# Six stage borders: the low part of the third tile's weights made by GpSimd in place of VectorE

## The chip, the cores and the metric

The kernel runs on one core of a Trainium2 chip. The metric is the device time of one launch in microseconds (us). Of the core's engines four compute here: TensorE (PE) multiplies matrices, VectorE (DVE), ScalarE (ACT) and GpSimd (POOL) work elementwise; SyncE (SP) issues transfers of weights. Each engine takes its instructions in order, and they wait for each other through semaphores.

## What is computed

Four layers of a diffusion backbone over 256 context and 256 latent tokens of 1024 features, in float32. Each layer has a token mixer (neighbourhood attention, retention, convolution, attention again) and a channel mixer, and ahead of each of these eight sub-layers stands a norm with a shift and a scale:

```python
for i in range(DEPTH):                       # 4 layers, D_MODEL = 1024
    hx = modulate_norm(xs, norm_mix[i], mx[0], mx[1])
    hc = modulate_norm(cs, norm_mix[i], mc[0], mc[1])
    yx, yc = mixer(hx, hc)                   # attention, retention or convolution
    xs = xs + mx[2] * yx
    hx = modulate_norm(xs, norm_ffn[i], mx[3], mx[4])
    xs = xs + mx[5] * conv_ffn(hx, ...)      # the same for cs, with mc
# modulate_norm: x * rsqrt(mean(x*x) + eps) * gain * (1 + scale) + shift
```

## The kernel before

**Products.** Features lie on the partitions, in 8 chunks of 128, and all 512 tokens in the columns: context CT (0 to 255), latent XT (256 to 511). For float32 precision each product is three: high weights by high activations (L718), high by low (L719), low by high (L720). The weights are streamed in groups of 128x1024 through four slots (`raw`, `Whi`). For each group ScalarE copies the rounded high part, Whi (L1230, semaphore `hi_split`), and VectorE subtracts it from the raw weights, Wlo (L1599, semaphore `lo_split`), in place: Wlo lies over raw. Both engines do so three groups ahead of TensorE (LEAD = 3). TensorE waits for `lo_split` ahead of each group.

**Borders.** A border is the change from one sub-layer's last projection to the next one's first tiles, with the residual sum and the norm between. Sub-layers are numbered r = 0 to 7. `HALVED = (0, 2, 1, 1, 1, 2, 1, 0)` says how many of the last output tiles of the projection ahead of r are made in halves, first all context columns, then the latent ones: it is so at the six borders r = 1 to 6. There the context tokens are normalised while TensorE still works on the latent halves.

TensorE (`last_halves`, then `three_tiles`): the next sub-layer's first two tiles for the context tokens, chunk by chunk (k = 0 to 7, six products of 256 columns each, each chunk behind `h_ready`); after k = 4 it sums the latent tokens' squares (`norm_sum`, L839 and L843), after k = 6 it spreads their roots over the partitions (`norm_spread`, L898), for which it needs VectorE's diagonal. Then it waits for `lo_split` of the third tile's weights, makes that tile for the context tokens, and goes on with the latent columns.

VectorE (`norm_halves`, `normed_chunks`): for each chunk c of a stream the product ring = X * scale * root (L1696, the root read from PSUM), and behind the product of chunk c + 1 the low part of chunk c, Hlo = ring + shift - Hhi (L1687, ring and Hhi in SBUF). Between the products of chunks 5 and 6 of the context tokens stands the split of the third tile's weights. Behind the context chunks come `invert_root(r, XT)` (reciprocal L1660, diagonal L1663) and the eight latent chunks.

ScalarE (`norm_apply`): the high parts Hhi (L1278) of chunks 2, 3, 4, then the high part of the third tile's weights, then the chunks 5 to 7 and the root of the sums (L1269).

GpSimd (`after_residual`): squares (L577) and adds up (L579) the chunks of X as they come; during the channel mixers of three layers it multiplies conditioning weights (`scale_weights`, L585), at the fourth border it goes on with filters of the convolution (`taps_diagonal`, L677), at the sixth with loads of the attention bias.

Of the kernel before, what the change touches and what calls it, by code (L numbers as in the profile page):

```python
# [24 lines left out]
F32 = mybir.dt.float32  # L25
F32R = mybir.dt.float32r
ALU = mybir.AluOpType
# [5 lines left out]
C = D // P  # L33
# [36 lines left out]
LEAD = 3  # L70
# [16 lines left out]
HALVED = (0, 2, 1, 1, 1, 2, 1, 0)  # L87
# [107 lines left out]
def build(nc, x, ada, weights, ada_in, ada_bias, gain, na_gain, rpb, na_mask, rope, decay, dist, gn_gain,  # L195
          cv_bias, cv_filter, quad, ffn_filter, ones, head_ones, identity, out):
    layers, n_groups = plan()
    ctx = ExitStack()
    with ctx:
        def sb(name, shape, dt=F32):  # L200
            return ctx.enter_context(nc.sbuf_tensor(name, shape, dt))

        def sem(name):
            return ctx.enter_context(nc.semaphore(name))
# [5 lines left out]
        Whi = sb("Whi", [P, SLOTS, GROUP], F32R)  # L210
# [3 lines left out]
        Wlo = sb("Wlo", [P, SLOTS, GROUP], F32R)  # L214
# [102 lines left out]
        x_loaded = sem("x_loaded")  # L317
        hi_split = sem("hi_split")
        lo_split = sem("lo_split")
        weights_used = sem("weights_used")  # L320
        tile_free = sem("tile_free")
        c_loaded = sem("c_loaded")
# [109 lines left out]
        def ctx_first(r):  # L432
            return sum(HALVED[:r])
# [5 lines left out]
        def norm_tokens(layer, part):  # L439

            return XT if layer == DEPTH - 1 and part == 1 else ALL
# [6 lines left out]
        def token_blocks(tok):  # L448
            return (2, 3) if tok == XT else (0, 1) if tok == CT else (0, 1, 2, 3)

        def spread_bank(r, tok):
            return bank[7 if HALVED[r] and tok == XT else 5]

# [10 lines left out]
        def weighed(n):  # L464
            return 2 * (n + 1) - shared_before(n + 1)
# [102 lines left out]
        def _(pool):  # L568
            g = nc.gpsimd

            def clear_total(r, tok):
                pool.wait_ge(norm_summed, upto(r - 1, XT))
                g.memset(total[:, tok], 0.0).then_inc(sum_step, 1)

            def add_square(r, nth, c, tok):

                g.tensor_tensor(square[:, c % 2, tok], X[:, c, tok], X[:, c, tok], ALU.mult).then_inc(sum_step, 1)  # L577
                pool.wait_ge(sum_step, sum_first(r) + 2 + 2 * nth)
                g.tensor_tensor(total[:, tok], total[:, tok], square[:, c % 2, tok], ALU.add).then_inc(sum_step, 1)  # L579

            def scale_weights(n, per=0, i=0):

                pool.wait_ge(cond_weighed, weighed(n) + per * i)
                w = cond_w[:, n % COND_SLOTS, :]
                g.tensor_tensor(w, w, cond[:, 0, :], ALU.mult).then_inc(cond_scaled, 1)  # L585

            def after_residual(r, tile0, tok):

                clear_total(r, tok)
                whole = C - 1 - (HALVED[r] == 2)  # L590
                for c in range(whole):
                    pool.wait_ge(tile_free, FREE0 + tile0 + 1 + c)
                    add_square(r, c, c, tok)
                if whole == C - 2:
                    pool.wait_ge(ctx_added, ctx_first(r) + 1)
                    add_square(r, whole, whole, CT)
                    pool.wait_ge(tile_free, FREE0 + tile0 + 1 + whole)
                    add_square(r, whole + 1, whole, XT)
# [47 lines left out]
            for layer, p in enumerate(layers):  # L646
                r = 2 * layer
                if layer % 3 == 0:
                    pairs_staged(layer)
                    out_tile = p["mix_tile"] + 24  # L650
                elif layer % 3 == 1:
                    def add(dst, a0, b0):
                        return g.tensor_tensor(dst, decay_t[:, 0, a0:a0 + CTX], decay_t[:, 1, b0:b0 + CTX], ALU.add)

                    for h in range(RET_HEADS):
                        if h:
                            pool.wait_ge(mask_made, 6 * h)
                        else:
                            pool.wait_ge(rope_step, 17)
                        g.dma_start(decay_t[:, :, :], dist).then_inc(dist_loaded, 16)  # L660
                        pool.wait_ge(decayed, 2 * h + 2)
                        for b, (left, right) in enumerate((((P, 3 * P), (3 * P, P)), ((0, 2 * P), (2 * P, 0)),
                                                           ((P, 3 * P), (0, 2 * P)))):
                            if h >= 2:
                                pool.wait_ge(ret_out, 3 * (h - 2) + b + 1)
                            add(A[h % 2][b][:, CT], *left).then_inc(mask_made, 1)
                            add(A[h % 2][b][:, XT], *right).then_inc(mask_made, 1)
                    pool.wait_ge(ret_out, 3 * RET_HEADS)
                    out_tile = p["mix_tile"] + 48
                else:  # L670
                    pool.wait_ge(norm_summed, upto(r, XT))
                    g.dma_start(quad_in[:, :], quad).then_inc(quad_loaded, 16)
                    g.memset(U[:, :, :, 0:CONV_PAD], 0.0).then_inc(pads_cleared, 1)
                    g.memset(U[:, :, :, CTX + CONV_PAD:], 0.0).then_inc(pads_cleared, 1)
                    pool.wait_ge(quad_loaded, 16)
                    for c in range(C):
                        g.tensor_tensor(taps_diagonal[:, c, :, :],  # L677
                                        quad_one.unsqueeze(1).to_broadcast([P, 4 * MOST, QUAD]),
                                        quad_w[:, c, :].unsqueeze(2).to_broadcast([P, 4 * MOST, QUAD]), ALU.mult)\
                            .then_inc(diag_made, 1)  # L680
                    for c in range(C):
                        for n in range(len(pool_taps[c]) - 1):
                            i = added_before[c] + n
                            pool.wait_ge(product_made, i + 1)
                            if n == 0:
                                pool.wait_ge(pool_begun, c + 1)
                            else:
                                pool.wait_ge(pool_added, i)
                            g.tensor_tensor(pooled[:, c % 2, :], pooled[:, c % 2, :], products[:, i % PRODUCTS, :],
                                            ALU.add).then_inc(pool_added, 1)  # L690
                    for c in range(1, 4):
                        pool.wait_ge(ln_square, c + 1)
                        if c > 1:
                            pool.wait_ge(ln_added, c - 1)
                        g.tensor_tensor(total[:, :], total[:, :], LN_SQUARES[c], ALU.add).then_inc(ln_added, 1)
                    pool.wait_ge(ln_used, 1)
                    out_tile = p["mix_tile"] + 16
                after_residual(r + 1, out_tile, norm_tokens(layer, 1))
                if p["hosts"]:
                    with pool.Fori(0, FC // 2) as i:  # L700
                        for q in range(PER_LAP):
                            scale_weights(p["cond_up"] + q, PER_LAP, i)
                if layer < DEPTH - 1:
                    after_residual(r + 2, p["down_tile"], ALL)


        @block.tensor
# [886 lines left out]
        def _(dve):  # L1594
# [7 lines left out]
            def split(st):  # L1602

                st = st.ahead(LEAD)
                if not isinstance(st.n, int) or st.n < n_groups:
                    split_group(st)
# [138 lines left out]
            def norm_halves(r, tiles, add_half, following):  # L1745


                for n, c in enumerate(tiles):
                    dve.wait_ge(ctx_made, ctx_first(r) + n + 1)
                    add_half(c, bank[c % 4], 0, CT, ctx_added)  # L1750
                if r % 2:
                    split(following[0])
                norm_scale(r)
                invert_root(r, CT)
                if len(tiles) == 2:
                    dve.wait_ge(weights_used, following[0].n + 1)
                    add_half(tiles[0], bank[7], 1, XT, tile_free)
                normed_chunks(r, 0, 0, 2)
                if r % 2 == 0:
                    split(following[0])  # L1760
                dve.wait_ge(weights_used, following[1].n + 1)
                add_half(tiles[-1], bank[6], 1, XT, tile_free)
                normed_chunks(r, 0, 2, 6)
                split(following[1])
                normed_chunks(r, 0, 6, C)
                invert_root(r, XT)
                normed_chunks(r, 1, 0, C)

# [546 lines left out]
```

## Time and profile before

| | us |
|---|---|
| median of three runs | 2487.61 (2486.81 to 2489.0) |
| the profiled run | 2486.94 |
| its span, first to last instruction | 2485.0 |

The page of the profile gives each engine's busy time and share of the span. The timeline lists instructions of one engine in order of time, with the idle time before each and the instruction that ended it. TensorE's granted clock stands at 9 tenths or more in all 40 slices of the page.

```profile
PEclk9999999999999999999999999999999999999999
```

### The profile page before, as it was taken

How to read it: one execution, taken by the hardware profiler on the slowest of the kernel's cores; microseconds unless marked ns; L12 is line 12 of the kernel's file. 1: busy time of each engine (PE TensorE's matmuls, PEld its weight loads, DVE VectorE, ACT ScalarE, POOL GpSimd, SP SyncE). 2: the span in 40 equal slices, each digit the busy share in tenths (PEclk: the TensorE clock that was granted, in tenths of full speed). 3: DMA queues.
4: the chain of work that ended last, by engine and by line, in shares of the span. 5: the costliest groups of instructions: out<-in, count | busy, mean ns of one | idle time of the engine just before them, and what ended most of it. 6: DMA issues, size and time to landing. Idle time of an engine off the chain costs nothing. (4 is left out here: it accounts for less than half of the span.)

```text
span 2485.0 us, 36153 instructions
## 1 busy us (share of the span) xinstructions
PE 2416.3 (97%) x12686; PEld 1979.5 (80%) x12686; DVE 1794.4 (72%) x2613; ACT 1019.5 (41%) x1545; POOL 639.1 (26%) x438
## 2 busy tenths in 40 slices
PE   7998899999999999999999998999999999998999
PEld 4675588888888878888888887668888888867999
DVE  4877569888974355427888777887988877855774
ACT  3335534443231244414444324654444324355543
POOL 2314233332200020032333225743333224101000
PEclk9999999999999999999999999999999999999999
DMA  8642025455632321233555543523544545312555
GB/s 280 178 166 72 10 85 174 172 170 193 217 112 93 112 75 51 95 100 136 169 177 169 178 153 119 146 64 129 179 164 161 190 165 136 111 43 78 186 185 178
DMA packets 105177, 346.23 MB, mean 139 GB/s; under 512 B 13904, under 2 KB 23904, under 8 KB 104944
## 3 DMA queue, kind: packets, MB, share of 16 engines
q1 hardware_dynamic: 74336, 246.48, 29.8%
q10 hardware_dynamic: 27808, 89.32, 11.0%
q0 software_dynamic: 2928, 9.00, 1.7%
q8 instruction: 70, 1.15, 0.2%
q14 instruction: 35, 0.29, 0.0%
HBM read 335.03 MB, written 1.05 MB: 135 GB/s over the span
## 5 line engine op out<-in xcount | busy, mean ns | idle before, releaser
L718 PE MATMUL bank<-Hhi,Whi 128*128 128x512 f32 (+1 forms) x2416 | 867.5, 359 | 26.6 <-DVE Wlo L1599 8.5
L720 PE MATMUL bank<-Hhi,Wlo 128*128 128x512 f32 (+1 forms) x2416 | 853.2, 353 | 0.0
L719 PE MATMUL bank<-Hlo,Whi 128*128 128x512 f32 (+1 forms) x2416 | 853.1, 353 | 0.0
L1599 DVE TENSOR_TENSOR Wlo<-raw,Whi 128x1024 fp32r<-128x1024 f32 x424 | 637.2, 1503 | 232.2 <-ACT Whi L1230 214.7
L1230 ACT ACTIVATE Whi<-raw 128x1024 fp32r<-128x1024 f32 x424 | 448.2, 1059 | 777.8 <-DMA raw<-in_weights 692.5
L718 PEld LDWEIGHTS bank<-Hhi,Whi 128*128 128x128 f32 x2416 | 457.2, 189 | 112.0 <-issue 36.3
L719 PEld LDWEIGHTS bank<-Hlo,Whi 128*128 128x128 f32 x2416 | 457.4, 189 | 63.6 <-issue 2.6
L720 PEld LDWEIGHTS bank<-Hhi,Wlo 128*128 128x128 f32 x2416 | 457.3, 189 | 62.3
L585 POOL TENSOR_TENSOR cond_w<-cond_w,cond 128x1024 f32<-128x1024 f32 x107 | 259.0, 2420 | 600.3 <-DVE square L1623 514.9
L718 PE MATMUL bank<-Ghi,Whi 128*128 128x512 f32 (+1 forms) x770 | 269.2, 350 | 0.0
L720 PE MATMUL bank<-Ghi,Wlo 128*128 128x512 f32 (+1 forms) x770 | 267.1, 347 | 0.0
L719 PE MATMUL bank<-Glo,Whi 128*128 128x512 f32 (+1 forms) x770 | 265.5, 345 | 0.0
L577 POOL TENSOR_TENSOR square<-X 128x512 f32<-128x512 f32 (+1 forms) x51 | 78.5, 1539 | 451.7 <-DVE X L1779 443.1
L720 PEld LDWEIGHTS bank<-Ghi,Wlo 128*128 128x128 f32 x770 | 144.6, 188 | 20.3
L719 PEld LDWEIGHTS bank<-Glo,Whi 128*128 128x128 f32 x770 | 144.5, 188 | 19.5
L718 PEld LDWEIGHTS bank<-Ghi,Whi 128*128 128x128 f32 x770 | 144.8, 188 | 17.4
L1623 DVE SCALAR_TENSOR_TENSOR hb<-cond_w,cond 128x1024 f32<-128x1024 f32 x113 | 153.5, 1358 | 3.8
L1537 ACT ACTIVATE hb<-hb 128x512 f32<-128x512 f32 (+1 forms) x88 | 51.0, 579 | 209.9 <-DVE hb L2141 209.8
L1623 DVE SCALAR_TENSOR_TENSOR square<-cond_w,cond 128x1024 f32<-128x1024 f32 x99 | 121.2, 1224 | 11.7
L1247 ACT ACTIVATE cond_w<-cond_w 128x1024 f32<-128x1024 f32 x107 | 112.5, 1051 | 37.5 <-POOL cond_w L585 36.8
L1834 DVE RECIPROCAL na_root<-na_root 128x512 f32<-128x512 f32 (+1 forms) x32 | 94.3, 2947 | 19.0 <-ACT na_root L1310 19.0
L1779 DVE SCALAR_TENSOR_TENSOR X<-bank,mod,X 128x256 f32<-128x256 f32 x84 | 37.4, 479 | 92.5 <-PE bank L720 92.3
(254 smaller groups left out, 2892.9 us busy)
## 6 DMA issues: line engine op xcount, KB each, us to landing
raw<-in_weights SPq DMA_DIRECT2D x424, 512.0 KB, 3.4
cond_w<-in_ada ACTq DMA_DIRECT2D x160, 512.0 KB, 4.0
ada_raw<-in_ada SPq DMA_DIRECT2D x16, 512.0 KB, 16.0
ada_ring<-in_ada SPq DMA_DIRECT2D x16, 512.0 KB, 7.2
rel_in<-in_rpb POOLq DMA_DIRECT2D x48, 128.0 KB, 4.9
shifted<-U SPq DMA_DIRECT2D x84, 66.0 KB, 2.1
decay_t<-in_dist POOLq DMA_DIRECT2D x4, 640.0 KB, 4.7
X<-in_x ACTq DMA_DIRECT2D x1, 2048.0 KB, 9.8
```

The lines of the kernel that those rows point to most:

```text
L577: g.tensor_tensor(square[:, c % 2, tok], X[:, c, tok], X[:, c, tok], ALU.mult).then_inc(sum_step, 1)
L585: g.tensor_tensor(w, w, cond[:, 0, :], ALU.mult).then_inc(cond_scaled, 1)
L718: t.matmul(dst, Whi[:, st.slot, w], hi, start=start, stop=False)
L719: t.matmul(dst, Whi[:, st.slot, w], lo, start=False, stop=False)
L720: return t.matmul(dst, Wlo[:, st.slot, w], hi, start=False, stop=stop)
L1230: a.activation(Whi[:, st.slot, :], raw[:, st.slot, :], ACT.Copy).then_inc(hi_split, 1)
L1247: a.activation(w, w, ACT.Copy, accum_out=cond_sum[:, n % COND_SLOTS, 0:1]).then_inc(cond_summed, 1)
L1537: a.activation(cv[:, k, tok], cv[:, k, tok], ACT.Gelu_apprx_tanh).then_inc(gelu_done, 1)
L1599: v.tensor_tensor(Wlo[:, st.slot, :], raw[:, st.slot, :], Whi[:, st.slot, :].bitcast(F32), ALU.subtract)\
L1623: last = v.scalar_tensor_tensor(scratch, w, 1.0, cond[:, r, :], ALU.mult, ALU.mult, accum_out=cond_sum[:, slot, r:r + 1])
L1779: last = v.scalar_tensor_tensor(X[:, m, hs], src[:, hs], gate, X[:, m, hs], ALU.mult, ALU.add)
L1834: v.reciprocal(na_root[:, m, tok], na_root[:, m, tok]).then_inc(qk_rstd, 1)
```

## The change

At each of the six borders the subtraction that makes the low part of the third tile's weights leaves VectorE's order and enters GpSimd's, behind the squares of that border. GpSimd waits for `hi_split` of that group alone and counts `edge_split` up. VectorE does the context chunks 2 to 7 in one go, then waits until `edge_split` has the count of this border and adds one to `lo_split`, which keeps counting the groups in their order. What TensorE and ScalarE do is unchanged.

```diff
+        edge_split = sem("edge_split")
...
+        def edges_upto(r):
+            return sum(1 for q in range(r + 1) if HALVED[q])
...
+            def edge_low(first):
+
+                st = Step(first + LEAD - 1)
+                pool.wait_ge(hi_split, st.n + 1)
+                g.tensor_tensor(Wlo[:, st.slot, :], raw[:, st.slot, :], Whi[:, st.slot, :].bitcast(F32), ALU.subtract)\
+                    .then_inc(edge_split, 1)
...
                 after_residual(r + 1, out_tile, norm_tokens(layer, 1))
+                if HALVED[r + 1]:
+                    edge_low(p["up"])
...
                     after_residual(r + 2, p["down_tile"], ALL)
+                    if HALVED[r + 2]:
+                        edge_low(layers[layer + 1]["mix"])
...
                 dve.wait_ge(weights_used, following[1].n + 1)
                 add_half(tiles[-1], bank[6], 1, XT, tile_free)
-                normed_chunks(r, 0, 2, 6)
-                split(following[1])
-                normed_chunks(r, 0, 6, C)
+                normed_chunks(r, 0, 2, C)
+                dve.wait_ge(edge_split, edges_upto(r))
+                dve.sem_inc(lo_split, 1)
                 invert_root(r, XT)
                 normed_chunks(r, 1, 0, C)
```

## Rows read from the trace of the kernel before

**Rows 1.** The page, part 1: busy time of each engine, share of the span, instructions.

```profile
PE 2416.3 (97%) x12686; PEld 1979.5 (80%) x12686; DVE 1794.4 (72%) x2613; ACT 1019.5 (41%) x1545; POOL 639.1 (26%) x438
```

**Rows 2.** One line's instructions: count, duration min/median/max in ns, first and last start.

```profile
L1599 DVE TENSOR_TENSOR Wlo<-raw,Whi x424: 1161/1224/3054, 28.2 to 2473.9; 128x1024 fp32r<-128x1024 f32 x142
...
L585 POOL TENSOR_TENSOR cond_w<-cond_w,cond x107: 2347/2406/3310, 168.5 to 1945.7; 128x1024 f32<-128x1024 f32 x107
```

**Rows 3.** Timeline, TensorE, first border: start, us, engine, line, out<-in, [idle before <-releaser].

```profile
340.51 0.59 PE L843 MATMUL bank<-one,root 128*128 128x2 f32 x4
340.96 0.36 PE L718 MATMUL bank<-Hhi,Whi 128*128 128x256 f32 x1
...
350.49 0.59 PE L843 MATMUL bank<-one,root 128*128 128x2 f32 x4
351.65 0.39 PE L718 MATMUL bank<-Hhi,Whi 128*128 128x256 f32 x1 [0.58 <-DVE Hlo L1687]
...
353.65 0.70 PE L898 MATMUL bank<-root,one 128*128 128x256 f32 x2 [0.24 <-DVE root L1663]
```

**Rows 4.** Timeline, VectorE, first border.

```profile
342.31 0.48 DVE L1771 SCALAR_TENSOR_TENSOR X<-bank,mod,X 128x256 f32<-128x256 f32 x1 [0.17 <-PE bank L720]
...
348.77 0.48 DVE L1687 SCALAR_TENSOR_TENSOR Hlo<-hb,mod,Hhi 128x256 fp32r<-128x256 f32 x1
349.59 1.23 DVE L1599 TENSOR_TENSOR Wlo<-raw,Whi 128x1024 fp32r<-128x1024 f32 x1 [0.34 <-ACT Whi L1230]
...
351.12 0.47 DVE L1687 SCALAR_TENSOR_TENSOR Hlo<-hb,mod,Hhi 128x256 fp32r<-128x256 f32 x1
...
351.91 0.47 DVE L1687 SCALAR_TENSOR_TENSOR Hlo<-square,mod,Hhi 128x256 fp32r<-128x256 f32 x1
352.57 0.48 DVE L1687 SCALAR_TENSOR_TENSOR Hlo<-square,mod,Hhi 128x256 fp32r<-128x256 f32 x1 [0.18 <-ACT Hhi L1278]
352.97 0.17 DVE L1660 RECIPROCAL token_root<-token_root 128x4 f32<-128x4 f32 x1
...
363.38 0.81 DVE L2136 TENSOR_SCALAR hb<-bank,fff 128x512 f32<-128x512 f32 x1 [2.05 <-PE bank L720]
```

**Rows 5.** Timeline, ScalarE, first border.

```profile
348.51 1.04 ACT L1230 ACTIVATE Whi<-raw 128x1024 fp32r<-128x1024 f32 x1
349.46 0.49 ACT L1278 ACTIVATE Hhi<-hb,mod 128x256 fp32r<-128x256 f32 x1
```

**Rows 6.** Timeline, GpSimd, first border, its last two operations.

```profile
342.88 0.61 POOL L577 TENSOR_TENSOR square<-X 128x256 f32<-128x256 f32 x1 [4.42 <-DVE X L1771]
343.57 0.75 POOL L579 TENSOR_TENSOR total<-total,square 128x256 f32<-128x256 f32 x1
```

**Rows 7.** Timeline, GpSimd and VectorE, inside the first channel mixer.

```profile
470.82 2.40 POOL L585 TENSOR_TENSOR cond_w<-cond_w,cond 128x1024 f32<-128x1024 f32 x1 [8.35 <-DVE square L1623]
...
471.29 3.01 DVE L1599 TENSOR_TENSOR Wlo<-raw,Whi 128x1024 fp32r<-128x1024 f32 x1
...
481.81 2.41 POOL L585 TENSOR_TENSOR cond_w<-cond_w,cond 128x1024 f32<-128x1024 f32 x1 [2.98 <-DVE square L1623]
...
482.52 2.77 DVE L1599 TENSOR_TENSOR Wlo<-raw,Whi 128x1024 fp32r<-128x1024 f32 x1 [0.20 <-ACT Whi L1230]
```

**Rows 8.** Timeline, GpSimd and VectorE, fourth border.

```profile
1508.93 9.20 POOL L677 TENSOR_TENSOR taps_diagonal<-quad_in 128x512 f32<-128x512 f32 x8 [1.44 <-DMA quad_in<-in_quad]
...
1511.58 0.88 DVE L1687 SCALAR_TENSOR_TENSOR Hlo<-hb,mod,Hhi 128x256 fp32r<-128x256 f32 x1
1512.38 0.47 DVE L1696 SCALAR_TENSOR_TENSOR square<-X,scale,bank 128x256 f32<-128x256 f32 x1
```

**Rows 9.** Timeline, VectorE, last of the six borders.

```profile
2072.43 1.23 DVE L1599 TENSOR_TENSOR Wlo<-raw,Whi 128x1024 fp32r<-128x1024 f32 x1 [0.34 <-ACT Whi L1230]
...
2073.97 0.48 DVE L1687 SCALAR_TENSOR_TENSOR Hlo<-hb,mod,Hhi 128x256 fp32r<-128x256 f32 x1
```

**Rows 10.** Timeline, TensorE, last of the six borders.

```profile
2074.50 0.38 PE L718 MATMUL bank<-Hhi,Whi 128*128 128x256 f32 x1 [0.59 <-DVE Hlo L1687]
```

## The prediction

> **What bounds the kernel now.** I read the page first: TensorE is busy for 97% of a span of 2485.0 us [rows 1], so a change elsewhere counts only where TensorE waits for it. The places are the six stage borders whose entry in HALVED isn't 0 (sub-layers 1 to 6). There I read the timelines of one border, engine by engine, always for the same question: which instruction ended just before TensorE started again.
>
> At the first border TensorE finishes the sums of squares of the latent tokens at 350.49 us and goes on at 351.65, after a wait that the row puts down to VectorE's Hlo (L1687). It then waits once more, for the diagonal, before the spread at 353.65 [rows 3]. The same steps without a wait, for the context tokens, stand 0.45 us apart (340.51 to 340.96) [rows 3]. So chunk 5 came 1.16 - 0.45 = 0.71 us late. VectorE's rows say why: low part of chunk 4 at 348.77, then the split of the third tile's weights at 349.59 (behind ScalarE's high part, which ends at 348.51 + 1.04 = 349.55), and only then the products of chunk 6 and, at 351.12, the low part of chunk 5 [rows 4, 5]. After that TensorE keeps VectorE's pace: low part of chunk 6 at 351.91, of chunk 7 at 352.57, the reciprocal for the latent tokens at 352.97, the spread 0.68 us behind it [rows 3, 4]. The latent halves are not what ends last: VectorE is done with them 2.05 us before 363.38, at 361.33, and idles until TensorE has finished [rows 4]. So every microsecond by which the low part of chunk 5 and the reciprocal move, moves the rest of the kernel. The last of the six borders has the same shape (split at 2072.43, low part of chunk 5 1.54 us later, TensorE at 2074.50 after 0.59 us) [rows 9, 10], and so have the four between.
>
> **What leaves.** Six splits of 1.22 us on VectorE [rows 2], and the wait of 0.34 us ahead of each [rows 4]. If nothing came in their place, the low part of chunk 5 would be held only by its high part on ScalarE, which the unmoved high split delays to 349.46 + 0.49 = 349.95 [rows 5]. It would start at 350.0 in place of 351.12.
>
> **What comes.** Six subtractions of 128x1024 on GpSimd. The same form of instruction there (two SBUF operands, result over the first) is L585: 2.35 us at least, 2.41 median, 3.31 at most [rows 2]. GpSimd has nothing else then: its last square ended at 344.3 [rows 6]. It waits for the high part alone, and starts 0.09 us after a release (342.31 + 0.48 = 342.79 against 342.88) [rows 4, 6]: 349.55 + 0.09 = 349.64. That a subtraction with an fp32r result costs what a multiplication costs there, no row shows; I take 2.41, the nearest, and 2.35 and 3.31 as bounds.
>
> **What the two do to each other** decides the case. At 470.82 GpSimd starts a multiplication; VectorE's split that starts at 471.29 takes 3.01 us instead of 1.22. At 481.81 the same again: 2.77 us from 482.52 [rows 7]. Taking the undisturbed 1.22 off the end of each, the splits really began at 471.29 + 3.01 - 1.22 = 473.08 and 482.52 + 2.77 - 1.22 = 484.07, both 2.26 us after GpSimd's start. So VectorE stood still for as long as GpSimd read, and this doesn't depend on when it came. It holds for the low parts too: beside GpSimd's eight operations of 9.20 us at 1508.93, L1687 takes 0.88 us instead of 0.48, while L1696, which reads one operand from PSUM, keeps its 0.47 [rows 8]. A low part reads ring and Hhi from SBUF.
>
> The Trainium skill says this as a rule (SBUF — State Buffer, "SBUF: two separate sides"): a VectorE instruction with two SBUF inputs and a GpSimd instruction that reads SBUF share a port pair under an exclusive lock, and the later one is blocked for the whole of the other. The trace agrees that it blocks and is a little milder on the length: 2.26 us of 2.41. By "the whole" the sum below would be 6 x 0.15 = 0.9 us higher, 2493.2.
>
> **The sum, at the first border.** GpSimd reads from 349.64 to 349.64 + 2.26 = 351.90. VectorE's steps of a chunk follow each other at 0.40 us (351.12 to 351.91 are two of them) [rows 4], so the products of chunk 6 come at 348.77 + 0.40 = 349.17, undisturbed. Its low part of chunk 5 can't start before 350.0, and finds GpSimd reading for 0.36 us already; it starts at 351.90, against 351.12 before: 0.78 us later. Low part 6 follows at 0.79 us, the high part of chunk 7 and its low part as before, so the reciprocal is at 353.75 instead of 352.97 and the spread 0.78 us later. TensorE waits 0.78 us longer at chunk 5. The new waits add nothing: GpSimd is done at 352.05, 1.7 us before VectorE comes to edge_split, and TensorE asks for lo_split of the third tile only behind chunk 7. Queued behind that wait on VectorE are the reciprocal, the diagonal and all latent halves, so it would be dear, but GpSimd's own reading holds VectorE up longer. The increment is one queue instruction; I take it at nothing, with 0.1 us a border as upper bound (VectorE's idle for a satisfied wait is hardly seen between 352.57 and 352.97 [rows 4]). Behind the borders GpSimd starts some 0.7 us later on what follows (the quad filter's load at the fourth, the bias loads at the sixth), the same shift as TensorE's. Nothing hides the 0.78 us, since TensorE has no other work in its order there.
>
> Six borders: 6 x 0.78 = **4.7 us longer**. Counted from 349.56, where the low part of chunk 5 would come if nothing held it, that is 1.56 us (split and wait) taken away at each border and 2.34 us of standing still put in its place. The profiled run took 2486.94 us and its span 2485.0, so the new span should be 2489.7; the profiled run is 0.7 us under the median of 2487.61. On the median the forecast is 2487.6 + 4.7 = **2492.3 us**. It follows the trace alone.
>
> **Rivals.**
> A. Collision as above: 2492.3, with the bounds 2.35 us and 0.1 us of queue from 2491.9 to 2492.9.
> B. GpSimd starts late. If it needs over 0.45 us from the release instead of 0.09, the low part of chunk 5 gets in first (350.0), TensorE has no wait there, and the reading falls on chunk 6: from 350.40 to 352.66, low part 6 then, low part 7 at 353.06, reciprocal at 353.45, 0.48 us later than before. 6 x 0.48 = 2.9: 2490.5. Against it speak the 0.09 us.
> C. No collision, because a low part of 256 columns slips between GpSimd's reads. Then the low part of chunk 5 starts at 350.0, TensorE goes on at 350.49 + 0.45 = 350.94, low part 7 is at 351.45, the reciprocal at 351.85, the spread 1.12 us earlier. 6 x 1.12 = 6.7: 2480.9. For it: VectorE really has 1.56 us less to do ahead of TensorE's wait. Against it: the rows at 1511.58, where just such low parts were held.
> D. Clearly slower: the subtraction with a rounded fp32r result takes GpSimd longer than L585. Each 0.1 us more is 0.1 us at each border, at any length, since VectorE stands for all of it. The line of 0.2% (5.0 us, 0.83 us a border) is passed from 0.05 us more on. At the maximum of 3.31 us: 6 x (0.78 + 0.90) = 10.1, 2497.7.
>
> **How the numbers follow.** A 0.60, B 0.11, C 0.14, D 0.15. The range should hold A, B and nearly all of D, which leaves out C: 2489.0 to 2497.5 us, about 0.83. About 0.2%, 5.0 us, is what a measurement of this kernel can tell from no change. Faster by more: C, 0.14. A lies just inside the line and small terms (queue, the longer lock) push it over, so I divide it 0.35 within and 0.25 beyond; with B within and D beyond: within 0.46, slower 0.40.
>
> **What the profile after would show.** VectorE at each border: no split between chunks 5 and 6, a first low part of about 2.38 us (350.0 to 352.38), in place of 0.48. GpSimd: one subtraction of about 2.4 us right behind the high split. TensorE: the wait at chunk 5 grows from 0.58 to about 1.36 us. If that low part is short and TensorE's wait is gone, C holds; if the long one is chunk 6's, B; if GpSimd's row is over 2.5 us, D. A reciprocal that starts behind GpSimd's end with VectorE idle before it would mean that edge_split ends last, which I exclude. The prediction is wrong if a later stage takes the 0.78 us up again, which would show as a border that is longer with the span unchanged.

## The result

| | before | changed |
|---|---|---|
| median, us | 2489.36 (10 runs, 2486.81 to 2492.47) | 2495.45 (10 runs, 2494.32 to 2500.1) |
| span of the profiled run, us | 2485.0 | 2493.1 |

The changed kernel takes 1.0026 times as long, with a 95% interval of 1.0016 to 1.0035: slower by some 6 us. The forecast was 2492.3, inside a range of 2489.0 to 2497.5; with more runs the kernel before stands at 2489.4 and not at 2487.6, so against the forecast of 4.7 us stand 6.1 us. The direction and the first cause were right, and a second cause was missing.

The page of the changed kernel, span and busy times. They say little: TensorE is busy 97% as before [rows 1], and GpSimd has six instructions more.

```profile
span 2493.1 us, 36159 instructions
...
PE 2423.5 (97%) x12686; PEld 1986.3 (80%) x12686; DVE 1794.6 (72%) x2607; ACT 1019.1 (41%) x1545; POOL 653.5 (26%) x444
```

GpSimd's new instruction (count, duration min/median/max in ns):

```profile
L589 POOL TENSOR_TENSOR Wlo<-raw,Whi x6: 2351/2354/2356, 350.6 to 2078.9; 128x1024 fp32r<-128x1024 f32 x6
```

The first border, to be read beside rows 3 to 6. First VectorE. These lines of the changed kernel are 15 further on than in the rows of before: L1702 is the low part, L1711 the product, L1675 the reciprocal.

```profile
349.71 0.48 DVE L1702 SCALAR_TENSOR_TENSOR Hlo<-hb,mod,Hhi 128x256 fp32r<-128x256 f32 x1
350.10 0.47 DVE L1711 SCALAR_TENSOR_TENSOR square<-X,scale,bank 128x256 f32<-128x256 f32 x1
350.93 2.28 DVE L1702 SCALAR_TENSOR_TENSOR Hlo<-hb,mod,Hhi 128x256 fp32r<-128x256 f32 x1 [0.35 <-ACT Hhi L1293]
353.13 0.47 DVE L1711 SCALAR_TENSOR_TENSOR square<-X,scale,bank 128x256 f32<-128x256 f32 x1
...
354.58 0.17 DVE L1675 RECIPROCAL token_root<-token_root 128x4 f32<-128x4 f32 x1
```

ScalarE and, under it, GpSimd:

```profile
349.45 1.04 ACT L1245 ACTIVATE Whi<-raw 128x1024 fp32r<-128x1024 f32 x1
350.40 0.49 ACT L1293 ACTIVATE Hhi<-hb,mod 128x256 fp32r<-128x256 f32 x1
```

```profile
350.57 2.35 POOL L589 TENSOR_TENSOR Wlo<-raw,Whi 128x1024 fp32r<-128x1024 f32 x1 [5.32 <-ACT Whi L1245]
```

TensorE, from the sums of squares to the spread:

```profile
351.42 0.59 PE L858 MATMUL bank<-one,root 128*128 128x2 f32 x4
353.26 0.39 PE L733 MATMUL bank<-Hhi,Whi 128*128 128x256 f32 x1 [1.25 <-DVE Hlo L1702]
...
355.27 1.22 PE L913 MATMUL bank<-root,one 128*128 128x256 f32 x2
```

ScalarE's high split ends at 349.45 + 1.04 = 350.49, and GpSimd starts 0.08 us later. VectorE has no split between the chunks any more. But its low part of chunk 5, released at 350.93, takes 2.28 us instead of 0.48. Taking the ordinary 0.48 us off its end, it really began at 350.93 + 2.28 - 0.48 = 352.73, 2.16 us after GpSimd's start. TensorE's wait at chunk 5 grew from 0.58 to 1.25 us.

The last row shows more. The spread takes 1.22 us for two instructions, where it took 0.70 [rows 3]. The same stretch in windows of 2 us (busy us and count of TensorE's products, its weight loads, VectorE, ScalarE, GpSimd, then the granted clock, DMA share, GB/s):

```profile
352.00:354.00 2.00, 0.74 (x7) 0.74 (x6) 2.00 (x3) 0.37 (x1) 0.92 (x1) 1.00 0.00 0
354.00:356.00 2.00, 2.00 (x12) 1.65 (x10) 1.00 (x3) 0.29 (x2) 0.00 (x0) 0.64 0.00 0
356.00:358.00 2.00, 2.00 (x11) 1.91 (x10) 1.29 (x4) 0.91 (x2) 0.00 (x0) 0.51 0.00 0
358.00:360.00 2.00, 2.00 (x18) 2.00 (x18) 2.00 (x7) 1.02 (x2) 0.00 (x0) 1.00 0.00 0
```

In the 2 us that hold the wait (352 to 354) TensorE was busy for 0.74 us. Soon after the wait its granted clock fell to half, the lower of its two levels (1.2 and 2.4 GHz), for some 3.4 us. Below this is called a fall. In the profiled run of before no border had this.

This table gives each border's length in us: from VectorE's reciprocal for the context tokens to TensorE's first product of 512 columns behind the border. A star marks a border with a clock fall behind chunk 5's wait. The last column is the sum of the differences to before. The labels are those of the experiments below; a_once_more is the changed kernel in another run.

| kernel | 1 | 2 | 3 | 4 | 5 | 6 | sum |
|---|---|---|---|---|---|---|---|
| before | 25.54 | 28.69 | 25.49 | 29.11 | 26.06 | 27.24 | |
| changed | 27.44* | 30.36* | 26.16 | 29.54 | 27.81* | 28.98* | +8.2 |
| changed (a_once_more) | 26.20 | 30.24* | 26.15 | 29.89 | 26.74 | 28.13 | +5.2 |
| e1_split_behind | 24.46 | 27.78 | 24.41 | 28.71 | 24.98 | 26.31 | -5.5 |
| e2_pool_writes_only | 24.41 | 27.67 | 24.36 | 28.33 | 24.93 | 26.59 | -5.8 |
| e3_keep_te_busy | 26.22 | 29.38 | 26.16 | 31.14 | 26.73 | 28.04 | +5.5 |
| e3_once_more | 26.21 | 29.44 | 26.19 | 30.56 | 26.74 | 28.07 | +5.1 |
| e4_wait_behind_diag | 27.20* | 29.43 | 26.15 | 29.52 | 27.82* | 28.97* | +7.0 |
| e5_both_behind | 24.43 | 27.71 | 24.38 | 29.15 | 24.93 | 26.14 | -5.4 |
| e6_pool_behind_diag | 25.77 | 27.64 | 25.71 | 28.62 | 26.28 | 27.76 | -0.4 |
| e7_taps_late | 24.44 | 27.64 | 24.43 | 26.97 | 24.98 | 26.18 | -7.5 |
| e8_half_each | 25.14 | 28.49 | 25.09 | 29.03 | 25.67 | 26.98 | -1.7 |
| e9_behind_and_taps | 24.42 | 27.84 | 24.38 | 26.77 | 24.95 | 26.17 | -7.6 |

The changed kernel's borders add up to 8.2 us more, beside a span that is 8.1 us longer. That the two agree so closely is chance: in a_once_more the borders give 5.2 us and the span (2495.1 us) 10.1 us. Of these, 4.3 us lie ahead of the first border, where the clock fell twice; such falls outside the borders differ from execution to execution. The third border, without a fall, is 0.67 us longer, the four with one 1.67 to 1.90 us.

### The profile page after: what moved, and what is told of

The parts are those of the page before. It is cut to its first block and busy times, and to the rows that moved or that the text cites. A ratio compares the mean times of both kernels' runs of the same rounds, so it can differ in the third digit from the quotient of the medians.

```text
span 2493.1 us, 36159 instructions
## 1 busy us (share of the span) xinstructions
PE 2423.5 (97%) x12686; PEld 1986.3 (80%) x12686; DVE 1794.6 (72%) x2607; ACT 1019.1 (41%) x1545; POOL 653.5 (26%) x444
## 3 DMA queue, kind: packets, MB, share of 16 engines
HBM read 335.03 MB, written 1.05 MB: 135 GB/s over the span
## 5 line engine op out<-in xcount | busy, mean ns | idle before, releaser
L1614 DVE TENSOR_TENSOR Wlo<-raw,Whi 128x1024 fp32r<-128x1024 f32 x418 | 627.5, 1502 | 235.8 <-ACT Whi L1245 217.6
```

The lines of the kernel that those rows point to most:

```text
L1614: v.tensor_tensor(Wlo[:, st.slot, :], raw[:, st.slot, :], Whi[:, st.slot, :].bitcast(F32), ALU.subtract)\
```

## The experiments

**GpSimd reads, or only writes (e2).** Theory: VectorE's low part is blocked because GpSimd reads from SBUF. Rival: any GpSimd work on that tile, or the new wait, costs. The kernel of this run fills the low part with zeros, so it leaves that part out of the products.

```diff
-                g.tensor_tensor(Wlo[:, st.slot, :], raw[:, st.slot, :], Whi[:, st.slot, :].bitcast(F32), ALU.subtract)\
-                    .then_inc(edge_split, 1)
+                g.memset(Wlo[:, st.slot, :].bitcast(F32), 0.0).then_inc(edge_split, 1)
```

> The changed kernel with a fill with zeros in place of GpSimd's subtraction, so the low part of the third tile's weights is left out of the products at the six borders; waits and signals are those of the changed kernel. GpSimd writes the same tile at the same time but reads nothing. Theory (GpSimd's reading blocks VectorE's low part): low part of chunk 5 takes 0.48 us instead of 2.28, reciprocal 1.1 us earlier than before, 6.7 us faster than the kernel before (ratio 0.9973), no fall of the clock. Rival (any GpSimd work on that tile, its write, or the new wait on VectorE costs): the low part stays near 2 us, or VectorE idles ahead of the reciprocal, ratio above 1.000.

Measured: 2483.54 us against 2488.5, ratio 0.9979 (0.997 to 0.9988). GpSimd, then VectorE at the first border:

```profile
352.01 0.95 POOL L589 MEMSET Wlo<- 128x1024 f32 x1 [5.30 <-ACT Whi L1244]
...
352.38 0.48 DVE L1701 SCALAR_TENSOR_TENSOR Hlo<-hb,mod,Hhi 128x256 fp32r<-128x256 f32 x1 [0.35 <-ACT Hhi L1292]
...
354.24 0.17 DVE L1674 RECIPROCAL token_root<-token_root 128x4 f32<-128x4 f32 x1
```

GpSimd's fill lies at 352.01 to 352.96, the low part of chunk 5 at 352.38 falls inside it and takes its ordinary 0.48 us. The new wait for edge_split is still there and costs nothing. So reading is what blocks. The Trainium skill (SBUF — State Buffer, "SBUF: two separate sides") limits the conflict to a GpSimd operation that reads SBUF, and the run agrees. The borders are 5.8 us shorter in sum: that is about what the cleared VectorE brings where the work costs nothing elsewhere.

**How long it blocks (e8).** GpSimd makes half of the columns, 512, and VectorE the other 512 behind the diagonal.

```diff
-                g.tensor_tensor(Wlo[:, st.slot, :], raw[:, st.slot, :], Whi[:, st.slot, :].bitcast(F32), ALU.subtract)\
+                w = slice(0, GROUP // 2)
+                g.tensor_tensor(Wlo[:, st.slot, w], raw[:, st.slot, w], Whi[:, st.slot, w].bitcast(F32), ALU.subtract)\
                     .then_inc(edge_split, 1)
...
                 normed_chunks(r, 0, 2, C)
-                dve.wait_ge(edge_split, edges_upto(r))
-                dve.sem_inc(lo_split, 1)
                 invert_root(r, XT)
+                dve.wait_ge(edge_split, edges_upto(r))
+                st, w = following[1].ahead(LEAD), slice(GROUP // 2, GROUP)
+                dve.wait_ge(hi_split, st.n + 1)
+                v.tensor_tensor(Wlo[:, st.slot, w], raw[:, st.slot, w], Whi[:, st.slot, w].bitcast(F32), ALU.subtract)\
+                    .then_inc(lo_split, 1)
```

> The changed kernel with GpSimd making the first 512 columns of the low part and VectorE the other 512 behind the diagonal. If VectorE is held for as long as GpSimd reads, the low part of chunk 5 takes 0.48 + 0.75 = about 1.2 us in place of 2.28, the reciprocal is 0.4 us earlier than before, and the border 0.3 to 0.4 us shorter than before (ratio 0.9992); the wait of TensorE at chunk 5 is short enough for the clock to stay. Rival (a fixed cost of handing over to GpSimd): low part near 2 us again, ratio 1.001 or more.

Measured: ratio 0.9995 (0.9986 to 1.0004). GpSimd, then VectorE:

```profile
349.43 1.28 POOL L590 TENSOR_TENSOR Wlo<-raw,Whi 128x512 fp32r<-128x512 f32 x1 [5.33 <-ACT Whi L1246]
...
349.78 1.21 DVE L1703 SCALAR_TENSOR_TENSOR Hlo<-hb,mod,Hhi 128x256 fp32r<-128x256 f32 x1 [0.35 <-ACT Hhi L1294]
...
352.37 0.17 DVE L1676 RECIPROCAL token_root<-token_root 128x4 f32<-128x4 f32 x1
```

The low part takes 1.21 us. It really began at 349.78 + 1.21 - 0.48 = 350.51, 1.08 us after a GpSimd instruction of 1.28 us. With 2.16 of 2.35 us above, the hold goes with GpSimd's length and ends 0.2 us before it. No fixed cost of handing over is seen. The borders are 0.1 to 0.4 us shorter than before, against 0.3 to 0.4 us expected.

**What the clock does (a_once_more, e3 twice).** The changed kernel again, and with ten small products on TensorE where it waits for chunk 5.

```diff
                     if r and k == 4:
                         norm_sum(r, XT)
+                        idle_products(10)
```

> The changed kernel with ten 128x128 products of the identity (about 0.13 us each by the rows at 2287.74) behind the sums of squares of the latent tokens, where TensorE waits for chunk 5. If TensorE's idle time is what lowers its clock at four borders, the granted clock stays at full speed in all six, the reciprocal stays 0.67 us later than before, and the kernel is 4.1 us slower than before (ratio 1.0016) in place of 6 to 8. Rival (the clock falls for another reason, as power): clock still falls to half for 3.4 us at four borders, ratio 1.0026 or more.

> The changed kernel once more, to see at how many borders TensorE's clock falls this time, and beside the next run on the same chip. By the theory (each border 0.67 us longer, each fall behind chunk 5's wait about 1 us more) with 2 to 5 falls: 6 to 9 us over the kernel before, ratio 1.0026. Rival (falls were a chance of the first looks): 0 or 1 fall, ratio 1.0016.

> The changed kernel with ten products of the identity on TensorE at chunk 5's wait, once more, beside the changed kernel on the same chip. Theory (idle time of TensorE is what lowers its clock there): no fall behind chunk 5's wait at any of the six borders again, the time 1.5 to 3 us under the changed kernel's. Rival: falls behind that wait as without the products, the same time as the changed kernel.

Measured: with the products 1.0018 (1.0009 to 1.0027) and 1.0017 (1.0008 to 1.0026); without them 1.0029 (1.0017 to 1.004) on the chip of the second. TensorE at the first border of e3_once_more:

```profile
351.59 0.59 PE L859 MATMUL bank<-one,root 128*128 128x2 f32 x4
352.04 1.29 PE L729 MATMUL bank<-ident 128*128 128x128 f32 x10
353.45 0.39 PE L733 MATMUL bank<-Hhi,Whi 128*128 128x256 f32 x1
```

The products fill 352.04 to 353.33, and chunk 5's follow at 353.45, where the changed kernel idled for 1.25 us. Over the two traces with them the clock fell behind this wait at none of 12 borders. Over the three traces in which the low part is equally late and TensorE idles (changed, a_once_more, e4) it fell at 8 of 18. In a_once_more it fell at one border only, which is the number of the rival in its expectation, while its time is that of the theory. In the eight traces where chunk 5 is less late it fell at none of 48.

The traces are one execution each; the granted clock, as a mean over an execution, is known for many more. Its average is 0.9936 in the 7 executions of a_once_more and 0.9955 in the 11 of e3_once_more, on the same chip. It is 0.9930 for the changed kernel (10 executions), 0.9943 for e4 (7), 0.9952 for e3_keep_te_busy (11), and 0.9953 to 0.9957 for the kernel before in three sets of 18 to 32 executions. So the products bring the clock back beyond the traced executions too. The ratios to the kernel before, with and without the products, overlap in their intervals. On the same chip the medians are 2492.89 and 2496.21 us, from 2488.94 to 2495.68 and from 2493.91 to 2499.34: the times support the reading, without proving it by themselves.

What makes a wait one behind which the clock falls is open. It isn't the length alone: TensorE idles 1.17 us at the start of the fifth border in all 13 traces, and up to 1.45 us at the end of the second (e1), and no fall followed. In e3_keep_te_busy one came at the fourth border, ahead of the products, behind a wait of 1.66 us. That border's 31.14 us are not the price of this fall: from the end of that wait to the reciprocal it takes as long as in the changed kernel, where no fall came (7.85 and 7.84 us). It is the wait that is 0.92 us longer than in the kernel before. The fourth border of e3_once_more has a wait of 1.06 us there and no fall; both are another 0.4 us longer behind the reciprocal, as in a_once_more, and why is open.

Where a fall follows chunk 5's wait it costs 0.8 to 1.2 us in the table: second border 30.24 against 29.43 in e4, first 27.44 against 26.20. The Trainium skill (Perfetto Trace Analysis, "Matmul Optimizations") says that the engine "dynamically scales power based on utilization, so it's important that matmuls execute back-to-back in batches". The 8 of 18 falls without the products and none of 12 with them agree; the waits without a fall show that not every gap costs.

**The new wait (e4).** VectorE's wait for edge_split moved behind the diagonal.

```diff
-                dve.wait_ge(edge_split, edges_upto(r))
-                dve.sem_inc(lo_split, 1)
                 invert_root(r, XT)
+                dve.wait_ge(edge_split, edges_upto(r))
+                dve.sem_inc(lo_split, 1)
```

> The changed kernel with VectorE's wait for edge_split and its increment of lo_split moved behind reciprocal and diagonal. Theory (the wait is over 1.7 us before VectorE comes to it): same time as the changed kernel, ratio 1.0026 within 0.0006, reciprocal 0.67 us later than before. Rival (the new wait or the queue instruction ahead of the reciprocal costs): reciprocal earlier by 0.1 to 0.7 us, ratio down to 1.001.

Measured: 1.0026 (1.0015 to 1.0038), the changed kernel's own ratio. On VectorE the same picture: 2.29 us, and the reciprocal 3.66 us behind the low part's start, as in the changed kernel (354.58 - 350.93 = 3.65).

```profile
351.33 2.29 DVE L1702 SCALAR_TENSOR_TENSOR Hlo<-hb,mod,Hhi 128x256 fp32r<-128x256 f32 x1 [0.35 <-ACT Hhi L1293]
...
354.99 0.17 DVE L1675 RECIPROCAL token_root<-token_root 128x4 f32<-128x4 f32 x1
```

**The split behind the diagonal (e1).** GpSimd makes nothing; VectorE's own split, from the kernel before, stands where VectorE idled until the spread.

```diff
-                normed_chunks(r, 0, 2, 6)
-                split(following[1])
-                normed_chunks(r, 0, 6, C)
+                normed_chunks(r, 0, 2, C)
                 invert_root(r, XT)
+                split(following[1])
                 normed_chunks(r, 1, 0, C)
```

> The kernel before, with VectorE's own split of the third tile's weights moved behind the diagonal of the latent tokens; GpSimd makes nothing. My theory (chunk 5 and the reciprocal set the border, GpSimd's reading holds VectorE): low part of chunk 5 at 350.0 behind its high part, reciprocal 1.1 us earlier, the split ends at about 353.7 just as TensorE comes to the third tile, so each border is 1.05 us shorter and the kernel 6.3 us faster than before (ratio 0.9975), with no fall of TensorE's clock. Rival (the border is bound by TensorE's own products or by the latent halves): no change, ratio 1.000, and TensorE's wait moves to the third tile.

Measured: 2483.69 against 2488.5 us, ratio 0.9981 (0.9972 to 0.999). VectorE, then TensorE:

```profile
351.62 0.48 DVE L1687 SCALAR_TENSOR_TENSOR Hlo<-hb,mod,Hhi 128x256 fp32r<-128x256 f32 x1 [0.35 <-ACT Hhi L1278]
...
353.48 0.17 DVE L1660 RECIPROCAL token_root<-token_root 128x4 f32<-128x4 f32 x1
...
354.03 1.22 DVE L1599 TENSOR_TENSOR Wlo<-raw,Whi 128x1024 fp32r<-128x1024 f32 x1
...
352.11 0.59 PE L843 MATMUL bank<-one,root 128*128 128x2 f32 x4
352.56 0.36 PE L718 MATMUL bank<-Hhi,Whi 128*128 128x256 f32 x1
```

Low part of chunk 5 in 0.48 us, split at 354.03 to 355.25, and TensorE goes on 0.45 us behind its sums, without a wait. Five borders are 0.9 to 1.1 us shorter, near the 1.05 expected; the fourth only 0.40. The whole is 4.8 us shorter where 6.3 were expected. The same 1.22 us of VectorE's work cost TensorE nothing at the new place. The reason for the change was sound; its target was not.

**GpSimd behind the diagonal (e6).** The changed kernel, with GpSimd waiting for VectorE's diagonal too, and TensorE for GpSimd. VectorE no longer waits for GpSimd.

```diff
                 st = Step(first + LEAD - 1)
+                pool.wait_ge(norm_diagonal, upto(r, XT))
                 pool.wait_ge(hi_split, st.n + 1)
...
                 pe.wait_ge(lo_split, steps[2].n + 1)
+                pe.wait_ge(edge_split, edges_upto(r))
                 third(CT)
...
                 normed_chunks(r, 0, 2, C)
-                dve.wait_ge(edge_split, edges_upto(r))
+                invert_root(r, XT)
                 dve.sem_inc(lo_split, 1)
-                invert_root(r, XT)
```

> GpSimd makes the low part as in the changed kernel, but starts only behind VectorE's diagonal; TensorE waits for GpSimd itself ahead of the third tile. Theory (it isn't GpSimd's 2.35 us that costs but what they collide with): chunk 5 as without any split, reciprocal 1.1 us earlier than before, the subtraction runs beside the first latent low part, which has slack, and TensorE gets its third tile about when it did before: ratio 1.000, 0 to 1 us, unless the clock falls at TensorE's wait of about 1.2 us there, which would add about 1 us for each fall. Rival (GpSimd at a border costs wherever it stands): ratio 1.0015 or more with the clock at full speed.

Measured: 0.9994 (0.9985 to 1.0003). GpSimd, VectorE and TensorE at the first border:

```profile
355.27 2.37 POOL L590 TENSOR_TENSOR Wlo<-raw,Whi 128x1024 fp32r<-128x1024 f32 x1 [8.24 <-DVE root L1680]
...
354.56 0.17 DVE L1677 RECIPROCAL token_root<-token_root 128x4 f32<-128x4 f32 x1
...
357.04 0.88 DVE L1704 SCALAR_TENSOR_TENSOR Hlo<-hb,mod,Hhi 128x256 fp32r<-128x256 f32 x1 [0.19 <-ACT Hhi L1295]
...
357.78 0.36 PE L734 MATMUL bank<-Hhi,Whi 128*128 128x256 f32 x1 [1.13 <-POOL Wlo L590]
```

The subtraction runs from 355.27 to 357.64. The first latent low part meets it and takes 0.88 us; TensorE isn't waiting for it. TensorE now idles 1.13 us for GpSimd itself at the third tile. So GpSimd at the border doesn't cost in itself, but at 2.35 us it is 1.1 us late for its reader. No fall followed in this trace at any of the six borders, though that wait is about as long as chunk 5's of 1.25 us, and the mean granted clock of the 11 executions, 0.9962, is no lower than before: why is open. The second and fourth borders came out 1.05 and 0.49 us shorter than before, which I had not expected. At the second, a wait of 1.19 us that the kernel before has at the border's end, for a later group's low part, is gone; the fourth was not followed up.

**ScalarE's split behind too (e5, e9), the filters later (e7).**

```diff
-                high(r, 0, 2, 5)
-                split(following[1])
-                high(r, 0, 5, C)
+                high(r, 0, 2, C)
                 root_of_norm(r, XT)
+                split(following[1])
                 high(r, 1, 0, C)
...
                     pool.wait_ge(quad_loaded, 16)
+                    pool.wait_ge(h_ready, p["mix_ready"] + 2 * C)
```

Both on top of e1: e5 has the first part, e7 the second, e9 both.

> The kernel with VectorE's split behind the diagonal, and ScalarE's high split of the same group moved too, behind the root of the latent tokens. Theory: the low parts of chunks 5 to 7 come 0.4 us earlier than with the split behind alone, but TensorE gets to chunk 5 only behind its sums, so the spread comes at most 0.1 us earlier, and the split ends no earlier (ratio to before 0.998, like the version with VectorE's move alone). Rival (the high part of chunk 5 on ScalarE is what ends last now): another 0.3 us a border, ratio 0.9972.

> The kernel with VectorE's split behind the diagonal, and GpSimd's eight filter operations of the fourth border held until the latent low parts are done. Theory: they stretch the latent low parts there from 0.48 to 0.88 us, TensorE waits for three of them; without that the fourth border is 1.0 us shorter than before in place of 0.4, another 0.6 us, which a whole time can hardly show. Rival: the filters come too late for the convolution and the gain is lost, the stage behind it longer.

> VectorE's and ScalarE's splits of the third tile behind the latent diagonal and root, and GpSimd's filters behind the latent low parts. Theory: the two steps of the earlier runs add, ratio 0.9973, no better than with ScalarE's split left where it is (0.9974). Rival: ScalarE's move helps once the fourth border is free, ratio under 0.9968.

Measured: e5 0.9984 (0.9975 to 0.9993), e7 0.9974 (0.9965 to 0.9984; 2480.72 against 2487.91 us), e9 0.9968 (0.9956 to 0.998; 2481.8 against 2488.71 us). ScalarE's move gives less than 0.2 us at any of the five borders and loses 0.4 us at the fourth. A collision of GpSimd's filters with the latent low parts stood there all along [rows 8]. TensorE at the fourth border of e1, waiting for latent low parts:

```profile
1514.94 0.39 PE L718 MATMUL bank<-Hhi,Whi 128*128 128x256 f32 x1 [0.21 <-DVE Hlo L1687]
...
1516.14 0.38 PE L718 MATMUL bank<-Hhi,Whi 128*128 128x256 f32 x1 [0.22 <-DVE Hlo L1687]
...
1517.33 0.39 PE L718 MATMUL bank<-Hhi,Whi 128*128 128x256 f32 x1 [0.22 <-DVE Hlo L1687]
```

And GpSimd and VectorE in e7, where the filters start behind the last low part and a low part takes 0.48 us:

```profile
1513.32 9.14 POOL L678 TENSOR_TENSOR taps_diagonal<-quad_in 128x512 f32<-128x512 f32 x8 [8.40 <-DVE Hlo L1688]
...
1511.23 0.48 DVE L1688 SCALAR_TENSOR_TENSOR Hlo<-hb,mod,Hhi 128x256 fp32r<-128x256 f32 x1
```

The fourth border went from 28.71 to 26.97 us. I had expected 0.6 us, the sum of the three waits shown, and this was too little: six of the eight latent low parts took 0.88 us in e1, and they followed each other at 1.19 us where they do so at 0.79 us in e7. TensorE, which needs them, comes to its next product of 512 columns 14.12 us behind the reciprocal instead of 15.74. e7 and e9, both faster than either kernel of the case, can't be told apart by these intervals; by the theory in the expectation of e9 their times are the same.

## Why the prediction was right, and where not

**What bounds the kernel**: right. e1 and e2 take the stall at chunk 5 away and the borders shrink by about the 1.05 and 1.12 us worked out (0.91 to 1.08 in e1, 1.02 to 1.13 at four borders in e2), except at the fourth, where the filters collide, and at the sixth in e2 (0.65), where an earlier wait of TensorE was 0.47 us longer.

**GpSimd's price and start**: right. 2.35 us was the lower bound of the prediction, 2.41 its value; the start came 0.08 us behind ScalarE, not 0.09. Rivals B and D are out.

**The collision**: right in mechanism at all six borders, a little smaller than its term: held 2.16 us and not 2.26, so the reciprocal came 0.67 us later (12.14 - 11.47 from the context reciprocal) and not 0.78. Six times that is 4.0 us instead of 4.7. The fourth border grew by only 0.43 us, but the collision cost it the same: TensorE's first wait there, ahead of all context chunks of the next tiles, happened to be 0.56 us instead of 0.74, and from its end to the reciprocal it takes 7.84 us instead of 7.17, again 0.67 more. Rival C would have needed an unheld low part.

**"The new waits add nothing"**: right (e4).

**The term that was missing**: the step "TensorE waits 0.78 us longer at chunk 5" took the wait at its own length. At 4 of 6 borders of the profiled run the clock fell behind it, 0.8 to 1.2 us each; with the products in the wait it fell at none of 12. In the whole time I put down to this the difference between 4.0 and the measured 6.1 us, which would be two falls in a typical execution. That number is not measured: the traces had 4, 3 and 1, and the mean clocks, with a fall of 3.4 us at half taking 1.7 us of full clock, would give between two and four more falls than before, an estimate.

**The number**: from the forecast of 2492.3 the base adds 1.75 us, the shorter hold takes 0.7 off, and the 2.1 us that are left to the measured 2495.45 I give to the falls. The errors went against each other in part. The measured time lies beyond rival A's upper bound of 2492.9, and the range held by luck: it reached up to 2497.5 for rival D, a slower GpSimd, which did not occur. The prediction had put A just inside the 0.2% line; the measured 0.26% is beyond it.

**The base**: the profiled run of before had no clock fall in its first 50 us, where ten of the twelve later traces had one (about 0.5 of full speed from 35 to 40 us in the changed kernel's), and its median of three runs was 1.75 us under that of ten.

## What to carry to other kernels

Before work is handed from VectorE to GpSimd, look for the instructions that VectorE issues meanwhile: those that read two operands from SBUF stood still here until 0.2 us before GpSimd's end, so the move traded VectorE's 1.22 us for a stretch of 2.16 us in which they could not begin. It costs less where VectorE is idle or reads one operand from PSUM [rows 8]. First try to move the work along its own engine's order to where that engine waits anyway: here this was worth 0.9 to 1.1 us at five borders, with nothing handed over. Look too for GpSimd work that already runs beside VectorE's critical steps: holding the filters back was worth 1.7 us at one border. And count with more than the length of a longer wait of TensorE, since the clock may fall behind it; which waits do this, the runs don't settle.

## What was not expected of the hardware

The granted clock fell behind a wait of 1.25 us at 8 of 18 such borders, from execution to execution at different ones, stayed at half for about 3.4 us, and cost 0.8 to 1.2 us. Behind waits of 1.13 us at six borders (e6) and 1.17 us at the fifth (all traces) it never fell. GpSimd's subtraction with an fp32r result takes the same 2.35 us as the quickest multiplication of that size, and its fill of the same tile 0.95 us without any hold on VectorE.
